# Loading and releasing every ring-home expert slab in halves, in all eight groups of both MoE layers

## What is computed

```python
def expert_block(args):                     # for every block of tokens of one expert
    toks, gts, e = args
    xb = h_pad[toks]
    u = jax.nn.silu(xb @ w_gate[e]) * (xb @ w_up[e])
    return (u @ w_down[e]) * gts[:, None]
```

## Time and profile before

| what | value |
|---|---|
| median of 3 runs | 2104.18 us (2103.56 to 2107.83) |
| the profiled execution: its own time | 2104.27 us |
| the profiled execution: span in the trace | 2102.5 us |
| TensorE busy (matmul rows) | 95% of the span |
| VectorE busy | 48% |
| ScalarE busy | 16% |
| moved by DMA | 625.56 MB, mean 298 GB/s |
| loads of ring slabs in halves | 64 DMAs of 1024 KB |

### The profile page before, as it was taken

How to read it: one execution, slowest core, us unless ns; L and a number is a source line. 1 busy time by engine, 2 the same in 40 slices (tenths; PEclk the granted TensorE clock), 3 DMA queues, 4 the chain that set the end, 5 groups by cost and what they waited for, 6 DMA issues and landing times.

```text
span 2102.5 us, 26759 instructions
## 1 busy us (share of the span) xinstructions
PE 2002.3 (95%) x11058; PEld 1345.8 (64%) x11058; DVE 1016.9 (48%) x1949; ACT 342.1 (16%) x755; POOL 0.2 (0%) x4
## 2 busy tenths in 40 slices
PE   8999999999999999999999989888999999998888
PEld 5999998999898999857734433333657544433333
DVE  5888864888573888355432222222356522222212
ACT  1443431000111000123200100000314100000000
POOL 0000000000000000000000000000000000000000
PEclk9999999999999999999999999999999999999999
DMA  8333436788446589443699999999934699999997
GB/s 332 127 145 121 160 142 252 255 317 321 147 164 237 206 319 336 148 153 111 273 392 426 428 426 427 428 428 425 390 129 185 251 416 427 428 425 428 427 429 321
DMA packets 118307, 625.56 MB, mean 298 GB/s; under 512 B 5808, under 2 KB 8496, under 8 KB 86192
## 3 DMA queue, kind: packets, MB, share of 16 engines
q1 hardware_dynamic: 117184, 619.06, 74.0%
q10 hardware_dynamic: 1008, 4.87, 0.6%
HBM read 622.86 MB, written 1.05 MB: 297 GB/s over the span
## 4 chain that ended last, share of the span: by engine, by line
PE 75%; DMA 17%; DVE 5%; ACT 1%; issue 1%; SPq 0%; DVEq 0%; ACTq 0%
PE ps L3025 14%; PE ps L2357 11%; PE ps L2383 8%; PE ps L2445 7%; PE ps L3059 7%; DMA ring<-in_w_up 5%; PE ps L2694 4%; DMA spare<-in_w_down 4%; DMA spare<-in_w_gate 4%; DMA spare<-in_w_up 4%; PE ps L2599 3%; PE ps L2687 3%; PE ps L2866 2%; PE ps L2640 1%; PE ps L2320 1%; PE ps L2518 1%
## 5 line engine op out<-in xcount | busy, mean ns | idle before, releaser
L3025 PE MATMUL ps<-ring,work_rows 128*64 128x512 f32 x1248 | 452.0, 616 | 29.1 <-DMA ring<-in_w_up 12.5
L3025 PEld LDWEIGHTS ps<-ring,work_rows 128*64 128x64 f32 x1248 | 140.2, 141 | 228.8 <-issue 225.5
L3025 PE MATMUL ps<-arena,work_rows 128*64 128x512 f32 x584 | 260.2, 597 | 16.7 <-DMA ring<-in_w_gate 9.2
L2357 PE MATMUL ps<-arena,ring 128*128 128x256 f32 x1024 | 224.7, 379 | 0.0
L3059 PE MATMUL ps<-ring,arena 128*64 128x512 f32 x608 | 212.3, 600 | 8.6 <-DMA spare<-in_w_down 3.7
L2357 PEld LDWEIGHTS ps<-arena,ring 128*128 128x128 f32 x1024 | 192.6, 189 | 27.4
L2445 PE MATMUL ps<-ring,work_rows 128*128 128x192 f32 x840 | 147.7, 327 | 0.4 <-ACT arena L947 0.4
L2142 DVE TENSOR_SCALAR arena<-arena 128x512 f32<-128x512 f32 x32 | 13.7, 427 | 277.8 <-ACT arena L1261 277.8
L2445 PEld LDWEIGHTS ps<-ring,work_rows 128*128 128x128 f32 x840 | 136.0, 190 | 1.5 <-issue 0.6
L3025 PEld LDWEIGHTS ps<-arena,work_rows 128*64 128x64 f32 x584 | 77.5, 136 | 91.7 <-issue 91.2
L3059 PE MATMUL ps<-arena 128*64 128x512 f32 x288 | 127.0, 594 | 6.2 <-DMA ring<-in_w_down 5.4
(11 more groups left out here) (447 smaller groups left out, 2654.3 us busy)
## 6 DMA issues: line engine op xcount, KB each, us to landing
ring<-in_mlp_w SPq DMA_DIRECT2D x32, 2048.0 KB, 13.0
ring<-in_w_up SPq DMA_DIRECT2D x32, 2048.0 KB, 34.8
ring<-in_w_gate SPq DMA_DIRECT2D x28, 2048.0 KB, 33.5
arena<-in_w_mod SPq DMA_DIRECT2D x24, 2048.0 KB, 8.2
ring<-in_w_down SPq DMA_DIRECT2D x24, 2048.0 KB, 35.3
arena<-in_w_gate SPq DMA_DIRECT2D x20, 2048.0 KB, 27.4
arena<-in_w_down SPq DMA_DIRECT2D x18, 2048.0 KB, 30.2
ring<-in_a_wqkv SPq DMA_DIRECT2D x23, 1536.0 KB, 6.8
```

The costliest lines, as they stand in the source:

```text
L2357: e = te.matmul(chunks(0, 8)[:, o, :], w[:, k, 128 * o:128 * o + 128], u3[j % 3][:, k, :], start=(start and k == 0 and o % 2 == 0), stop=F ...
L3025: e = te.matmul(bank(b)[SB * h:SB * h + SB], xs(k, col, SB), slabs.chunk(m + h, k), start=(k == 0), stop=(k == KD - 1), skip_group_check=True)
```

## The change

`HALVED` becomes all 96 slabs of a layer. Since only slabs in ring homes count (`SLOT[n] < SLOTS`), 58 slabs per layer are halved where 16 were: 42 more per layer, all of them among slabs 24 to 91. The slabs beside the ring stay whole. Loads, waits and releases of the newly halved slabs follow the rules told above. The other edits (`LAST_BESIDE`, which is empty, and the renamed helpers) give the same semaphores and counts as before.

```diff
--- before.py
+++ after.py
@@ -93,7 +93,8 @@
 GATE_AT, UP_AT, DOWN_AT = (0, 4), (2, 6), (8, 10)
 PART_OF = (0, 0, 1, 1, 0, 0, 1, 1, 2, 2, 2, 2)
 EXPERT_OF = (0, 1, 0, 1, 2, 3, 2, 3, 0, 1, 2, 3)
-HALVED = tuple(range(2 * GROUP_SLABS)) + tuple(range(HOME_SLABS - 4, HOME_SLABS))
+HALVED = tuple(range(HOME_SLABS))
+LAST_BESIDE = {}
 MIDDLE = NG // 2
 FILL = 2
 
@@ -164,7 +165,8 @@
 
 
 SLOT, BEFORE, COUNT = slab_slots()
-HALVED_SLABS = {n for n in (lay * LAYER + MOE + m for lay in range(DEPTH) for m in HALVED) if SLOT[n] < SLOTS}
+HALVED_SLABS = {n for n in (lay * LAYER + MOE + m for lay in range(DEPTH) for m in HALVED)
+                if SLOT[n] < SLOTS or (n - MOE) % LAYER in LAST_BESIDE}
 
 
 def is_halved(n):
@@ -177,9 +179,14 @@
     return sum(m <= n for m in HALVED_SLABS)
 
 
-def halved_in_slot(n):
-
-    return sum(m <= n and SLOT[m] == SLOT[n] for m in HALVED_SLABS)
+def half_signal(n):
+
+    return LAST_BESIDE.get((n - MOE) % LAYER, SLOT[n])
+
+
+def halved_before(n):
+
+    return sum(m <= n and half_signal(m) == half_signal(n) for m in HALVED_SLABS)
 
 
 class Ring:
@@ -218,7 +225,7 @@
         eng.wait_ge(self.landed[SLOT[n]], (turns + COUNT[n]) * (32 if SLOT[n] == ONCE else 16))
 
     def wait_half_landed(self, eng, n):
-        eng.wait_ge(self.half_landed[SLOT[n]], halved_in_slot(n) * 16)
+        eng.wait_ge(self.half_landed[half_signal(n)], halved_before(n) * 16)
 
     def wait_done(self, eng, n, turns=0):
         eng.wait_ge(self.done, turns * SLOTS + n + 1)
@@ -770,7 +777,7 @@
 
                     n, src = slab(m)
                     ring.wait_half_free(sp, n)
-                    sp.dma_start(ring.tile(n)[:, 0:HALF], src[:, 0:HALF]).then_inc(half_landed[SLOT[n]], 16)
+                    sp.dma_start(ring.tile(n)[:, 0:HALF], src[:, 0:HALF]).then_inc(half_landed[half_signal(n)], 16)
 
                 def load_rest(m):
```

## The result

The changed kernel took 2114.72 us (median of 8 runs, 2111.03 to 2116.42) against 2105.39 us before (8 runs, 2103.56 to 2108.97). The ratio is **1.0039, 95% interval 1.0031 to 1.0048**: slower by 8.2 us (6.5 to 10.1). Forecast were +8.5 us, 2112.7 us, and slower by over 0.2% with a chance of 0.70. The absolute time is 2.0 us above the forecast; 1.2 of that is the base, which the forecast took as 2104.2.

The account below looks back on a forecast made before the run. The prediction took each layer to be bound by the landing of slab 93 in a full DMA queue, then TensorE's last work. From 2104.2 us, +7.1 - 1.0 + 2.4 = +8.5 gave 2112.7 us, range 2106.2 to 2116.3.

Parts of the forecast that it names:

- What bounds: Both MoE layers: the DMA queue is full, and slab 93's landing, then TensorE's last work, bounds a layer.
- More transfers: Full DMA queue ahead of slab 93: 84 slabs as two 1 MB transfers cost 0.085 us each, +7.1 us.
- The tail: Last ups, slabs 90 and 91: halving wins only slab 93's lead over the downs in layer 1, -1.0 us.
- The clock: Ahead of each layer's last downs: TensorE idles about 4.3 us and its clock falls, 1.2 per layer, +2.4 us.
- Waits, counts, issues at nothing: TensorE's second waits and counts and SP's 84 more issues are hidden by slab waits and queue backlog: nothing.
- That an earlier release gains nothing: Places given out sooner: a load issued 3.5 us sooner only waits 3.5 us longer in the queue, no gain.
- The sum: Whole kernel: +7.1 - 1.0 + 2.4 = +8.5 us, so 2112.7 us, +0.4%.
- Within 0.2%: Rival, whole kernel: low transfer price, no clock cost, full tail gain, +4.8 or +3.1 us, within 4.2; chance 0.23.
- Faster: Rival, wait ahead of the last downs: last part ends 3.5 us sooner per layer, 2097 us; chance 0.06.
- The dry queue: Rival, groups 2 to 7: SP issues late once per group, 12 x 2.4 = 29 us, 2142 us; chance 0.04.

Follow-up runs that it names:

- e6: The kernel before, with the 84 slabs each fetched by one DMA in 2 rows of 8 KB per partition instead of one of 16 KB; 2112.78 us, ratio 1.0028.
- e7: The kernel before, with the 84 slabs each fetched by one DMA in 4 rows of 4 KB per partition; 2125.17 us, ratio 1.0089.
- e1: The changed kernel, but slabs 90 and 91 whole again in both layers; 2111.34 us, ratio 1.0029 to the kernel before.
- e2: The kernel before, but with slabs 90 and 91 halved in both layers; 2109.93 us, ratio 1.0013.
- e8: The changed kernel, but a first half is issued only when the whole old slab is used; 2121.65 us, ratio 1.0073 to the kernel before.
- e10: The kernel before, with slabs 12 to 23 (group 1) whole; 2107.9 us, ratio 1.0010.
- e9: The kernel before, with slabs 90 to 93 halved too in both layers; 2105.69 us, ratio 0.9997.
- e4: The changed kernel, but the 84 newly halved slabs cut by partitions (0 to 63, 64 to 127) instead of columns; 2791.37 us, ratio 1.301 to the kernel before.

## Why the prediction was right, step by step

*What bounds.* That a layer ends behind the landing of slab 93 held: its landing and the start of the downs are 0.14 us apart in both layers, and the 3.2 us of each layer's landing went to the end undiminished.

*More transfers:* +7.1 forecast (0.085 a slab), +6.4 in the trace, 6.3 by the 0.075 that e6 and e7 bear out. The value was between the two measured stretches, and the lower one (0.07, at the end of a layer) was the better: the other was read from times rounded to 0.1 us. I had counted the price by transfers and had not asked whether rows or transfers cause it; the sum didn't depend on it. The two figures that the prediction took from the Trainium skill, "DMA: Bandwidth & Descriptors", for comparison are given there for transfers that GpSimd issues, and the loads here are issued by SP; that they don't hold in this queue says nothing against them.

*The tail:* -1.0 forecast. In layer 1 the lead of 0.9 to 1.0 us is gone; the stage's +0.8 is 1.7 of clock less 0.9.

*The clock:* +2.4 forecast, +3.4 in the trace. Direction and place were right, both sizes off. The wait was put at 4.3 us and was 2.1 and 2.3: I let the last up part end 3.6 us behind the landing of slab 91, but TensorE was still behind with the slabs ahead of it and ended that part later (transpose done at 1468.9, 7.8 us behind slab 91, not 5.6). And I discounted the loss to 1.2 a layer where it was the full 1.7 each time. That waits of 2 us so close to the downs would cost as much was not to be had from the earlier trace rows, where equal waits went either way; e1 and e2 show it by taking the wait out and putting it in. Here I had luck: by my own rows a wait of 2.2 us was an even chance of losing the clock, and I expected the loss nearly always only because I had put the wait at twice its length.

*Waits, counts, issues at nothing:* borne out by e6, which has no more of them than the kernel before and the same loss as e1, and by groups 2 and 3 of the changed kernel. (Group 1 has seven halved slabs, not eight; that doesn't change the term.) An issue on SP, put at 0.33 to 0.43 us, takes 2 us and more in the full queue; the backlog hides it, as said, but its price was not the one that I gave. That an earlier release gains nothing holds for the full queue alone: at the start of a layer it is worth some 3 us (e8), which changed nothing in the sum, as those slabs were released early before, too.

*The sum:* +8.5 against +8.75 in the trace. It came nearer than its terms: the price was 0.7 us too high, the clock 1.0 too low.

*The rivals.* "Within 0.2%" failed by the transfers alone: without the clock term the change would be e1, +6 us, which is over 4.2 already, as was the rival's own sum of +4.8; it needed a price of 0.05 a slab, and that was 0.075. "Faster" failed for the reason given, slab 93, and e2 shows it was a trap: the shorter part turned into a wait. The dry queue did not come.

## What to carry to other kernels

Where a queue is full from end to end, count bytes and rows, not issue times: cutting a load there buys neither an earlier start nor an earlier finish, and shorter rows have a price that is exposed in full. Cut loads only where the queue runs dry (here at the start of a layer: e8, and e10 as far as its small effect goes) or where the consumer follows the very last landing, and there cut all slabs that it waits for, else the time won in front of the next whole slab is idle time that TensorE pays for with its clock (e2 against e9).

## What the runs showed of the hardware

Each DMA engine pays 9 ns more for each further row into which the same bytes are cut, at rows of 16, 8 and 4 KB, whether they come in one transfer or in two (e6, e7 and the changed kernel).

A queue with transfers into 64 partitions in it runs at half the rate, 209 against 424 GB/s, with the DMA engines busy (e4). The Trainium skill, "DMA: Bandwidth & Descriptors", section "Rules for kernel authors", advises against cutting by partition halves because the two serialize; the run shows a loss of half the rate on top.

SP is held up when many rows are outstanding. SP's own timeline in the changed kernel, in group 3 of layer 0, with the time each issue took:
```profile
1228.21 2.10 SPq L701 DMA_DIRECT2D arena<-in_w_up  x1
1230.36 2.14 SPq L701 DMA_DIRECT2D ring<-in_w_up  x1
1232.55 0.43 SPq L780 DMA_DIRECT2D ring<-in_w_gate  x1
1233.78 7.94 SPq L701 DMA_DIRECT2D ring<-in_w_gate  x1
1241.77 2.13 SPq L701 DMA_DIRECT2D spare<-in_w_gate  x1
```
Before, issues of slabs mostly took 0.33 to 0.43 us. The issues of ups into ring homes in 1200 to 1440 (shortest, median and longest, in ns), in the kernel before, the changed one, e6 and e7:
```profile
L694 SPq DMA_DIRECT2D ring<-in_w_up x11: 327/431/433, 1225.7 to 1424.3; - x11
```
```profile
L701 SPq DMA_DIRECT2D ring<-in_w_up x11: 328/2136/6572, 1230.4 to 1431.6; - x11
```
```profile
L700 SPq DMA_DIRECT2D ring<-in_w_up x11: 367/2440/7359, 1228.8 to 1431.8; - x11
```
```profile
L700 SPq DMA_DIRECT2D ring<-in_w_up x10: 1081/4512/13962, 1241.9 to 1439.8; - x10
```
It is the rows that count, not the transfers. The kernel before has up to nine slab loads outstanding and is hardly held up; e6 has no more than nine and e7 no more than eight, and both are. When an issue that took over 1 us ended, the median number of other slab loads outstanding was 9 in the changed kernel, 6 in e6 and 4 in e7; by the rows of each that is 72, 80 and 88 to 96 rows per DMA engine, the part of the oldest load that had already been moved included. The kernel before has the same elsewhere: behind loads with rows of 2 KB, at 1503.51, the issue of a slab took 5.29 us. Here this costs nothing, as the queue is still some 30 us ahead (28 in e7); a kernel that needs one queue to be both long and finely cut would meet it.
